# Query blocks from long to short in three attentions, and a mask added by two products in rounded type

## What is computed

```
hybrid layer (twice):   x = x + 0.5 * swiglu(rmsnorm(x))
                        z = rmsnorm(x) @ w_in
                        y = [attention A (top-k of 128 keys, distance bias), gated linear attention B,
                             convolution C, causal attention D]  @ w_out ;  x = x + y
                        x = x + 0.5 * swiglu(rmsnorm(x))
even layer:             q, k, v, u = rms_norm(x) @ w_in
                        att = dilated_attention(rope(q) / 8, rope(k), v)      8 heads of 64
                        ssm = s5_mixer(u)
                        x = x + rms_norm([att, ssm] @ w_out) ; then a feed-forward network
odd layer:              a gated linear recurrence, then a feed-forward network
```

## Time and profile before

| | us |
|---|---|
| median of 3 runs | 3611.69 (3611.07 to 3620.76) |
| profiled execution, own time | 3610.73 |
| its span in the profile | 3609.0 |
| PE busy | 3435.9 (95%) |
| VectorE busy | 1590.3 (44%) |
| ACT busy | 1169.3 (32%) |
| POOL busy | 455.2 (13%) |

### The profile page before, as it was taken

How to read it: one execution, slowest core, us unless ns; L and a number is a source line. 1 busy time by engine, 2 the same in 40 slices (tenths; PEclk the granted TensorE clock), 3 DMA queues, 4 the chain that set the end, 5 groups by cost and what they waited for, 6 DMA issues and landing times.

```text
span 3609.0 us, 39889 instructions
## 1 busy us (share of the span) xinstructions
PE 3435.9 (95%) x14476; PEld 2608.8 (72%) x14476; DVE 1590.3 (44%) x2269; ACT 1169.3 (32%) x1722; POOL 455.2 (13%) x319
## 2 busy tenths in 40 slices
PE   7999998899999999999899999899899997889998
PEld 5888773678887788775577888566678886568886
DVE  3332587434323433287534332834343326454322
ACT  4232344433322332244334321213333213543322
POOL 1110003111100110001211110401011003321100
PEclk9999998899999999999799999899999999899999
DMA  4332320023333333331013333331133332223332
GB/s 134 97 94 93 83 81 31 1 70 93 93 95 95 90 93 93 93 80 63 1 36 92 94 93 93 88 79 43 47 87 93 94 94 64 70 70 93 96 96 76
DMA packets 420124, 286.04 MB, mean 79 GB/s; under 512 B 57416, under 2 KB 395180, under 8 KB 419884
## 3 DMA queue, kind: packets, MB, share of 16 engines
q1 hardware_dynamic: 419200, 283.62, 27.3%
q10 hardware_dynamic: 828, 1.13, 0.1%
HBM read 280.24 MB, written 4.47 MB: 79 GB/s over the span
## 4 chain that ended last, share of the span: by engine, by line
PE 88%; DVE 7%; ACT 2%; issue 2%; POOL 0%; DMA 0%; DVEq 0%; ACTq 0%; SPq 0%; POOLq 0%
PE bank L845 25%; PE bank L846 25%; PE bank L847 24%; PE bank L1229 1%; PE bank L1112 1%; PE bank L1113 1%; PE bank L1131 1%; PE bank L840 1%; PE bank L1223 1%; DVE arena L2010 1%; DVE small L2008 1%; PE bank L943 0%; PE bank L1089 0%; DVE w_lo L1911 0%; PE bank L980 0%
## 5 line engine op out<-in xcount | busy, mean ns | idle before, releaser
L847 PE MATMUL bank<-xn_lo,w_hi 128*128 128x512 f32 x2800 | 1098.3, 392 | 0.0
L845 PE MATMUL bank<-xn_hi,w_hi 128*128 128x512 f32 x2496 | 1000.4, 401 | 58.9 <-DVE xn_lo L1900 20.1
L1911 DVE TENSOR_TENSOR w_lo<-wring,w_hi 128x1024 fp32r<-128x1024 f32 x476 | 593.3, 1248 | 918.2 <-ACT w_hi L1477 917.2
L846 PE MATMUL bank<-xn_hi,w_lo 128*128 128x512 f32 x2496 | 990.9, 397 | 0.0
L1477 ACT ACTIVATE w_hi<-wring 128x1024 fp32r<-128x1024 f32 x490 | 517.5, 1059 | 1191.8 <-DMA wring<-in_ffn_down 357.8
L847 PEld LDWEIGHTS bank<-xn_lo,w_hi 128*128 128x128 f32 x2800 | 529.3, 189 | 132.7
L845 PEld LDWEIGHTS bank<-xn_hi,w_hi 128*128 128x128 f32 x2496 | 470.9, 189 | 181.4 <-issue 63.7
L846 PEld LDWEIGHTS bank<-xn_hi,w_lo 128*128 128x128 f32 x2496 | 471.9, 189 | 104.1 <-issue 1.7
L846 PE MATMUL bank<-h_hi,w_lo 128*128 (+1 forms) x1056 | 420.4, 398 | 0.0
L845 PE MATMUL bank<-h_hi,w_hi 128*128 (+1 forms) x1056 | 415.8, 394 | 0.0
L847 PE MATMUL bank<-h_lo,w_hi 128*128 (+1 forms) x1056 | 415.2, 393 | 0.0
(11 more groups left out here) (372 smaller groups left out, 3053.4 us busy)
## 6 DMA issues: line engine op xcount, KB each, us to landing
wring<-in_ffn_gate SPq DMA_DIRECT2D x88, 512.0 KB, 3.8
wring<-in_ffn_up SPq DMA_DIRECT2D x88, 512.0 KB, 3.8
wring<-in_ffn_down SPq DMA_DIRECT2D x88, 512.0 KB, 3.5
wring<-in_ffn_w_gate SPq DMA_DIRECT2D x44, 512.0 KB, 3.8
wring<-in_ffn_w_up SPq DMA_DIRECT2D x44, 512.0 KB, 3.8
wring<-in_ffn_w_down SPq DMA_DIRECT2D x44, 512.0 KB, 3.6
wring<-in_w_in SPq DMA_DIRECT2D x34, 512.0 KB, 3.7
wring<-in_w_out SPq DMA_DIRECT2D x16, 512.0 KB, 4.9
```

The lines of the kernel that those rows point to most:

```text
L845: nc.tensor.matmul(ps, w_hi[:, slot, t, 0:M], hi, start=start, stop=False)
L846: nc.tensor.matmul(ps, w_lo[:, slot, t, 0:M], hi, start=False, stop=False)
L847: return nc.tensor.matmul(ps, w_hi[:, slot, t, 0:M], lo, start=False, stop=stop)
L1911: nc.vector.tensor_tensor(w_lo[:, slot, :, :].rearrange("p k c -> p (k c)"), wunit[:, slot, :], w_hi[:, slot, :, :].rearrange("p k c -> p ...
```

## The change

First, the lists of units count the query blocks down: in each head the block with 512 keys comes first and the one with 128 last. The waits that belong to the first unit of a head (`hyb_ready`, `even_ready`) move to the block `tb == TB - 1`. The order in which POOL prepares the masks of type A follows from the same list.

Second, the even attention adds its table by two products in fp32r. Ahead of the attention ACT writes an identity matrix in fp32r (`one_r`) and the rounded table (`ln_hi`), VectorE the rest (`ln_lo` = table - `ln_hi`). Each unit then adds `one_r` x `ln_hi` and `one_r` x `ln_lo` where it added `ident` x table. The first unit waits for `ln_split`. To free a semaphore for this, the last transposes count on `pro_ps` instead of a semaphore of their own.

```diff
+        ln_hi, ln_lo = [nc.alloc_sbuf_tensor_at(n, [P, SEQ], F32R, offset=at["arena"] + t * SEQ * 4)
+                        for n, t in (("ln_hi", 22), ("ln_lo", 23))]
+        one_r = nc.alloc_sbuf_tensor_at("one_r", [P, P], F32R, offset=at["arena"] + 24 * SEQ * 4)
...
-        D_UNITS = [("D", h, tb) for h in range(D_HEADS) for tb in range(TB)]
-        A_UNITS = [("A", h, tb) for h in range(A_HEADS) for tb in range(TB)]
+        D_UNITS = [("D", h, tb) for h in range(D_HEADS) for tb in reversed(range(TB))]
+        A_UNITS = [("A", h, tb) for h in range(A_HEADS) for tb in reversed(range(TB))]
...
-                    msk, lo = ops["mask"](m, h, tb, i)
+                    masks, lo = ops["mask"](m, h, tb, i)
...
-                    nc.tensor.matmul(s[:, lo:N], ident, msk, start=False, stop=True).then_inc(att_s.h, 1)
+                    for n, (one, msk) in enumerate(masks):
+                        mm = nc.tensor.matmul(s[:, lo:N], one, msk, start=False, stop=(n == len(masks) - 1))
+                    mm.then_inc(att_s.h, 1)
...
-        E_UNITS = [("E", h, tb) for h in range(E_HEADS) for tb in range(TB)]
+        E_UNITS = [("E", h, tb) for h in range(E_HEADS) for tb in reversed(range(TB))]
...
+        def even_mask(m, h, tb, u):
+            return [(one_r[:, :], t[:, SEQ - (tb + 1) * P:]) for t in (ln_hi, ln_lo)], 0
...
+            nc.scalar.activation(one_r[:, :], ident, ACT.Copy)
+            nc.scalar.activation(ln_hi[:, :], C("lnmult"), ACT.Copy).then_inc(tab_sin.h, 1)
...
-                act.e.wait_ge(fin_ps.h, n + 1)
+                act.e.wait_ge(pro_ps.h, 2 + KD + 4 + A_HEADS + n + 1)
...
+            dve.e.wait_ge(tab_sin.h, 5)
+            tt(ln_lo[:, :], C("lnmult"), ln_hi[:, :].bitcast(F32), ALU.subtract).then_inc(ln_split.h, 1)
```

More of the change, by code:

```diff
@@ L617, in program @@
         y_lru = sem("y_lru")
-        fin_ps = sem("fin_ps")
+        ln_split = sem("ln_split")
         fin_sb = sem("fin_sb")
-        D_UNITS = [("D", h, tb) for h in range(D_HEADS) for tb in range(TB)]
-        A_UNITS = [("A", h, tb) for h in range(A_HEADS) for tb in range(TB)]
+        D_UNITS = [("D", h, tb) for h in range(D_HEADS) for tb in reversed(range(TB))]
+        A_UNITS = [("A", h, tb) for h in range(A_HEADS) for tb in reversed(range(TB))]
         HYB_UNITS = D_UNITS + A_UNITS
@@ L1151, in hyb_mask @@
             if m == "D":
-                return C("causal"), tb * P
+                return [(ident, C("causal"))], tb * P
             if tb == 0:
-                return bias[:, h, SEQ - P:SEQ], 0
-            return T(t_bm[BM.index(u) % 3])[:, 0:(tb + 1) * P], 0
+                return [(ident, bias[:, h, SEQ - P:SEQ])], 0
+            return [(ident, T(t_bm[BM.index(u) % 3])[:, 0:(tb + 1) * P])], 0
         def hyb_v(m, h, b):
@@ L1168, in hyb_ready @@
             m, h, tb = HYB_UNITS[u]
-            if m == "D" and tb == 0:
+            if m == "D" and tb == TB - 1:
                 eng.e.wait_ge(dh_ready.h, dh_ready.by(eng.l, 5 + h))
-            if m == "A" and h == 0 and tb == 0:
+            if m == "A" and h == 0 and tb == TB - 1:
                 eng.e.wait_ge(mn_x.h, mn_x.by(eng.l, 4))
@@ L1195, in even_ready @@
                 eng.e.wait_ge(glu_sb.h, 4)
+                eng.e.wait_ge(ln_split.h, 1)
             m, h, tb = E_UNITS[u]
-            if tb == 0 and h % 2 == 0:
+            if tb == TB - 1 and h % 2 == 0:
                 eng.e.wait_ge(rot_ready.h, 2 * (h // 2) + 2)
@@ L1200, in even_ready @@
                 eng.e.wait_ge(ez_sb.h, len(E_Z))
-        EVEN = dict(qk=even_qk, mask=lambda m, h, tb, u: (C("lnmult")[:, SEQ - (tb + 1) * P:], 0),
+        def even_mask(m, h, tb, u):
+            return [(one_r[:, :], t[:, SEQ - (tb + 1) * P:]) for t in (ln_hi, ln_lo)], 0
+        EVEN = dict(qk=even_qk, mask=even_mask,
                     v=lambda m, h, b: e_vv[:, b, h * E_DIM:(h + 1) * E_DIM], ready=even_ready)
@@ L1419, in _ @@
                     mm = nc.tensor.transpose(pb[FIN_BANKS[n % 4]][:, k * P:(k + 1) * P], x[:, 4 * q + k, tb * P:(tb + 1) * P], ident)
-                mm.then_inc(fin_ps.h, 1)
+                mm.then_inc(pro_ps.h, 1)
         LN_EXP = "natural_log_exp_and_others"
```

## The result

| | before | after |
|---|---|---|
| median, us (20 runs each) | 3613.50 (3610.43 to 3621.44) | 3630.33 (3614.21 to 3665.03) |
| ratio to before, 95% interval | | 1.0043 [1.0031, 1.0054] |
| profiled execution, own time | 3610.73 | 3634.95 |
| its span | 3609.0 | 3633.2 |
| granted PE clock, mean over the span | 0.969 | 0.956 |

The account below looks back on a forecast made before the run. PE was taken to bound the kernel, busy 3435.9 of 3609.0 us. Masks 10.1 plus order 7.3 gave 17.4 us off 3610.7: 3593.3, or 3594.3 us on the scale of medians; range 3588 to 3602 us.

Parts of the forecast that it names:

- New wait: 1.7 us there, 1.1 us in the even one: Before unit 12's V product, PE waits for ACT's extra work: 1.7 us in a hybrid attention, 1.1 in the even.
- a stretch at the low clock that moves: Example of something outside the forecast case and its rivals; no place or size given, chance 0.02.
- the same 4 us: Start of a hybrid attention: the 4 us at the low clock stay the same in either order.
- Masks, forecast 10.1 us: Even attention: two rounded-type mask products per unit cost 1.32 us a head, not 2.59; gain 10.1 us, bounds 3.3 to 12.8.
- my slope: Mask product time from 0.232 us at 512 columns: one column per clock plus 0.02 us, giving 0.18 at 384, 0.13 at 256.
- Order, forecast 7.3 us: All three attentions, long blocks first: less PE waiting, 2.7 us per hybrid and 1.9 in the even; bounds 1.5 to 10.
- waits of 0.50 and 0.83 us a head: Ascending order: PE's loss per head behind 512 columns, 0.83 in first-type heads; forecast gone, or about 0.1 in hybrid's first four.
- thin margins: Even attention, descending: PE's cover exceeds the chain through VectorE and ACT by only 0.1 to 0.2 us; 0.35 us allowed for failures.
- Preparation, forecast nothing: Before the even attention: two ACT copies and one VectorE subtraction for the mask halves cost nothing; without cover, 1.6 us.
- A: Rival: order pays nothing, PE waits as often behind ACT's extra work; gain 12 us at most, 3600 us; chance 0.10.
- B: Rival, dear short mask products: at old type's price 3601.1 us; with 0.05 us exposed weight load each 3597.5; chance 0.11.
- C: Rival: even attention's mask pair costs two old-type matmuls, 20.7 us more, less the order's 7.3: 3625 us; chance 0.03.

Follow-up runs that it names:

- filled kernel: Changed kernel plus two useless float32 products before unit 15's scores in each attention, where PE stood idle: 3600.21 us, ratio 0.9954 to the kernel before.
- spread kernel: Changed kernel with ACT's weight units every fourth step, pair copies two steps later, VectorE's extra work likewise: 3590.38 us, ratio 0.9935 to before; repeat 3592.94 us.
- light descending attention: Spread kernel with two useless ACT copies before the head copy of step 17 in the even attention: 3619.09 us, ratio 0.9980 to the kernel before.
- ascending float32 one: Kernel before with one useless ACT copy before the head copy of step 19 in the even attention: 3614.56 us, ratio 0.9994.

## Why the prediction was wrong

The result was the opposite of the forecast, from one step: **"New wait: 1.7 us there, 1.1 us in the even one"**. The wait came, at the unit that I had named and with nearly that size (688.85 and 1806.07 us: 1.35 listed and 0.16 for the drain, 1.51; 2510.56 us: 1.08). But I priced it as idle time and nothing more. It is followed by a fall of the granted clock, and that costs 97.70 - 69.21 = 28.5 us in the even attention (against the filled kernel) and 78.88 - 69.92 = 9.0 us in the second hybrid one (against the first). Taken from the profiled execution, in which these two falls stand: 3635.0 - 37.5 = 3597.5 us, where my sum for such an execution was 3593.3. The filled kernel, with its clock kept, measured 3600.2 us. Both lie within my range, so without the fall the sum would have held, if 4 to 6 us too low. I had looked at the clock before, at 1.00 in the earlier trace rows, and carried it over to a kernel with other waits; "a stretch at the low clock that moves" got a chance of 0.02, and the granted clock stood in my text only as a sign of being wrong. What I should have asked: before, PE had no gap over 0.83 us inside an attention but one at its very end (2551.42 us: 1.17 listed, with the wide products of the projection 4 us behind), so no row says what a gap of 1.1 or 1.5 us does with 20 units of short products still to come. Even the gap at the end was not safe: later traces show a fall of 6.8 us behind 2 of 14 of them. That the low level at the start of a hybrid attention is "the same 4 us" was not exact either: in the traces here it lasts 3.4 to 6.4 us, so a difference of two hybrid attentions is good to about 1.5 us.

The single terms:

- **Masks, forecast 10.1 us.** Two products of each width cost 0.57, 0.45, 0.34 and 0.28 us (from start to start, at 2494.85 to 2500.59 us in the changed kernel), 1.64 a head instead of my 1.32. Gain (2.59 - 1.64) x 8 = 7.6 us; the mask alone measured 7.0 us in the even attention and 8.1 us in the median. The first product of a pair, which follows a float32 matmul, is dearer by 0.06 to 0.10 us than the second; my slope came from a row in which this type follows itself. Inside my bounds.
- **Order, forecast 7.3 us.** The spread kernel's attentions are 2.9, 4.0 and 12.0 us shorter than before's, 18.9 us together; less 7.6 for the masks, 11.3 us. With my new waits taken out, which that kernel doesn't have (1.7 + 1.7 + 1.1 = 4.5 us), I would have had 7.3 + 4.5 = 11.8. The waits of 0.50 and 0.83 us a head went, as forecast, and so did the end: 0.47 us listed before the last transposes, once. The thin margins held; no head's third or fourth unit waits. The waits of 0.4 us that I had given to the pair's copies at steps 21 and 29 and to VectorE's weight units are not in the changed kernel's list for the even attention.
- **Preparation, forecast nothing.** The first scores wait 0.69 us for ACT's L1763, as they did before; the two new copies show in no wait.
- **Rivals.** A (order pays nothing) is refuted by the changed kernel's own list, one wait at the V products of the even attention where there were seven, and by the spread kernel's 11.3 us from the order. B's first form (dear short products, 3.3 us) is refuted by the 7.6 us of the masks. Its second form, 0.05 us more on every product and so 6.9 us of gain, came closer in size than my 10.1; the extra stands at the first product of each pair. C (slower by the price of the products) is refuted by the mask alone, 0.9977. The result was slower for a reason that was no rival of mine.

The Trainium skill ("TensorE: Matmul & The Clock Gate", section "A second HAM failure mode: psum-queue depth-cycling") tells of a kernel in which PE's very short idle times between groups of matmuls make its clock swing between the two levels. This case's traces agree in kind: single gaps of 0.85 to 2.6 us were followed by the lower level. They differ in one thing: here one gap inside an attention was enough, and the low level then stayed for 17 to 68 us with PE busy nearly throughout.

**Open.** Why a gap of one length is followed by a fall in one execution and not in the next; what sets the chance besides the length (0.69 us listed: 6 of 10 in the light descending attention; 0.86: 0 of 11 in the ascending float32 one; 1.35: in three traces the second hybrid attention each time and the first never, though both run the same code); and why the heads with wide float32 masks brought the clock back after 20 to 31 us in four traces and only after 48 us in another. How many falls each of the unprofiled executions had is read from their mean clocks alone.

## What to carry to other kernels

Price a new wait of TensorE in a stretch of short or narrow products twice: its own time, and the time until the next wide products at half the clock, with a chance that here grew with the gap. When engines beside it have extra work, spread it one piece a step over the loop rather than in a row, even if its sum hides easily; here this turned 1.0043 into 0.9935. If PE must wait there, useless products in the gap can be cheaper than the gap (here by 30 us), and a median with two clusters behind it is to be read execution by execution, with the clock beside each time.

## What was not expected of the hardware

- The granted clock fell within an attention some 0.8 to 2.6 us behind the end of an idle time of PE of 0.85 to 1.54 us, in part of the executions, and behind 2.6 us in all 6 (by their times and mean clocks). Behind the 1.17 us listed at the end of an ascending attention it fell in 2 of 14 places in the traces.
- It stayed at 0.50 for 68 us with PE busy 63.62 of 64 us, on matmuls over 64 rows, blocks of 64 columns and short products; 8 float32 products of 512 columns brought it back after some 2.8 us.
- At the low level a head took 14.9 us (2541.96 to 2556.84 us) instead of 8.08, 1.84 times, not twice.
- A rounded-type product of 128 columns behind a float32 matmul took 0.17 us, behind one of its own type 0.11; at 512 columns 0.33 and 0.24.
